# A decoder trunk on one core: projection pieces gathered behind Y, selection rounds shifted into the recurrence

## The reference

```
x = x + 0.5 * swiglu(rms_norm(x))
h = rms_norm(x); P = h @ W_in          # split by columns into the groups' q, k, v, ...
A: sparse attention, 6 heads x 64: index scores, top-128 keys per query, softmax with bias
B: gated delta rule, 6 heads x 64, chunks of 64 tokens, convolution, decay, output norm
C: attention into 256 memory tokens, 4 heads x 64
x = x + concat(A, B, C) @ W_out
x = x + 0.5 * swiglu(rms_norm(x))
```

```
v_new = u - w @ S;  o = q @ S + attn @ v_new;  S = decay * S + k^T @ v_new
```

## Time and profile before

| what | us |
|---|---|
| median of 3 runs (lowest to highest) | 2200.27 (2198.32 to 2202.68) |
| the profiled execution: its time | 2206.89 |
| its span, first to last instruction | 2205.1 |
| TensorE busy | 2179.1 (99%) |
| VectorE busy | 1079.1 (49%) |
| ScalarE busy | 772.6 (35%) |
| GpSimd busy | 380.1 (17%) |

### The profile page before, as it was taken

The page is one execution under the profiler, slowest core; times in us unless marked ns, Lnnn a source line. Parts: engine busy times, 40 slices in busy tenths (PEclk is TensorE's granted clock), DMA queues, the critical chain, the costliest instruction groups (busy, mean ns, idle before and its releaser), DMA issues.

```text
span 2205.1 us, 33287 instructions
## 1 busy us (share of the span) xinstructions
PE 2179.1 (99%) x13849; PEld 1762.6 (80%) x13849; DVE 1079.1 (49%) x1481; ACT 772.6 (35%) x1046; POOL 380.1 (17%) x319
## 2 busy tenths in 40 slices
PE   9999999999999999999999999999999999999999
PEld 7888888777777888888888888887777778888887
DVE  5333333789747544343343333338796465333322
ACT  5222223474335332222232222234743353222211
POOL 0111012005223410101111110120141134111000
PEclk9999999999999999999999999999999999999999
DMA  5222233221011222223222222232211012322232
GB/s 189 95 95 95 88 105 112 97 96 32 31 67 39 77 96 95 95 90 105 93 96 97 99 103 89 93 128 80 93 41 60 29 39 77 114 95 95 91 101 76
DMA packets 30651, 192.43 MB, mean 87 GB/s; under 512 B 3216, under 2 KB 5392, under 8 KB 11984
## 3 DMA queue, kind: packets, MB, share of 16 engines
q1 hardware_dynamic: 30160, 189.80, 25.5%
q10 hardware_dynamic: 384, 1.07, 0.1%
HBM read 188.64 MB, written 2.10 MB: 86 GB/s over the span
## 4 chain that ended last, share of the span: by engine, by line
PE 90%; DVE 7%; ACT 2%; issue 1%; DMA 0%; SPq 0%; DVEq 0%; ACTq 0%
PE psum L872 26%; PE psum L874 26%; PE psum L873 26%; PE psum L1290 2%; PE psum L1152 1%; PE psum L1003 1%; PE psum L1274 1%; PE psum L1167 1%; DVE wl L1707 1%; PE psum L1263 1%; DVE acc L1790 1%; PE psum L1237 1%; PE psum L1205 1%; DVE XL L1722 1%; PE psum L1199 1%
## 5 line engine op out<-in xcount | busy, mean ns | idle before, releaser
L872 PE MATMUL psum<-XH,wh 128*128 128x512 f32 x1904 | 764.2, 401 | 4.9 <-DVE wl L1707 1.8
L874 PE MATMUL psum<-XH,wl 128*128 128x512 f32 x1904 | 744.5, 391 | 0.0
L873 PE MATMUL psum<-XL,wh 128*128 128x512 f32 x1904 | 744.0, 391 | 0.0
L872 PEld LDWEIGHTS psum<-XH,wh 128*128 128x128 f32 x1904 | 358.7, 188 | 94.2 <-issue 14.8
L874 PEld LDWEIGHTS psum<-XH,wl 128*128 128x128 f32 x1904 | 358.8, 188 | 75.9
L873 PEld LDWEIGHTS psum<-XL,wh 128*128 128x128 f32 x1904 | 359.1, 189 | 73.8 <-issue 4.3
L1715 DVE TENSOR_TENSOR wl<-raw,wh 128x2048 fp32r<-128x2048 f32 x88 | 201.8, 2293 | 159.4 <-ACT wh L1360 159.4
L872 PE MATMUL psum<-HH,wh 128*128 128x512 f32 x704 | 273.9, 389 | 0.0
L873 PE MATMUL psum<-HL,wh 128*128 128x512 f32 x704 | 273.9, 389 | 0.0
L874 PE MATMUL psum<-HH,wl 128*128 128x512 f32 x704 | 273.9, 389 | 0.0
L1355 ACT ACTIVATE wh<-raw 128x2048 fp32r<-128x2048 f32 (+1 forms) x84 | 157.3, 1872 | 307.5 <-PE psum L874 307.3
(11 more groups left out here) (256 smaller groups left out, 2143.4 us busy)
## 6 DMA issues: line engine op xcount, KB each, us to landing
raw<-weights SPq DMA_DIRECT2D x143, 1024.0 KB, 5.0
raw<-weights SPq DMA_DIRECT2D x32, 896.0 KB, 4.6
xT<-xt SPq DMA_DIRECT2D x4, 512.0 KB, 6.6
memT<-memt SPq DMA_DIRECT2D x2, 1024.0 KB, 4.9
out<-xT SPq DMA_DIRECT2D x8, 256.0 KB, 5.8
stripsA<-strip_table SPq DMA_DIRECT2D x2, 768.0 KB, 6.8
raw<-weights SPq DMA_DIRECT2D x2, 512.0 KB, 6.8
stripsB<-strip_table SPq DMA_DIRECT2D x2, 512.0 KB, 7.4
```

The source lines that it names most:

```text
L872: pe.matmul(out_ap, a_hi, b_hi, start=first, stop=False)
L873: pe.matmul(out_ap, a_hi, b_lo, start=False, stop=False)
L874: return pe.matmul(out_ap, a_lo, b_hi, start=False, stop=last)
```

## The change

Only `_order` changes. In the Y and X steps `pull` is now called with 2.04 behind Y and not at all behind X; it was called with 1.02 behind each (behind "w" it stays 1.02). A selection round stands behind X and W, where it stood behind each step of Y, X and W but the last four. Eight rounds are thus fewer in the inversion; they stand in the recurrence behind each r1, which is behind the scaled values U on VectorE. As `later` counts calls of `pull`, the steps of the head norms and splits move too: they stand behind Y steps and W only.

```diff
--- before.py
+++ after.py
@@ -311,16 +311,18 @@
 
     for i, step in enumerate(INVERSION):
         order.append(step)
-        if i < len(INVERSION) - 4 and step != ("kq", 2):
+        if i < 9 and step != ("kq", 2) or step[0] in ("x", "w"):
             sel(1)
         if i < 9:
             pull(0.7 if i < 6 else 1.3)
-        else:
-            pull(1.02)
+        elif step[0] != "x":
+            pull(2.04 if step[0] == "y" else 1.02)
         if i == 0:
             put(("vt", 2), ("vt", 3))
     for step in RECURRENCE:
         order.append(step)
+        if step[0] == "r1":
+            sel(1)
         if step in FILLED:
             pull(0.92)
     assert all(name == "v" and b == 3 for name, b, _, _ in fill) and not later
```

## The result

The changed kernel took 2207.51 us (median of 10 runs, 2203.14 to 2213.93), the kernel before beside it 2200.16 (10 runs, 2198.32 to 2203.24): a ratio of 1.0027, 95% interval 1.0017 to 1.0036. The time lies inside the range of 2196 to 2209, but not at 2201.8: the difference was +7.35 us where +1.5 was forecast, and by the bound of 0.2% the kernel is slower, a case that had a chance of 0.15. The forecast's own range ended at 2205.5; the part above it, in which the measured time lies, was there for rival B, which did not happen. Two later timings of the same code gave 1.0021 (1.0013 to 1.0030) and 1.0014 (1.0003 to 1.0025).

What follows compares the result with a forecast made beforehand. TensorE bounds it, 90% of the chain. 18.7 (Y) + 29.9 + 4.3 + 18.6 + 0.6 + 7.0 = 79.1 us against 78.73 and 78.32; +1.5 us with g): 2201.8. Own range 2198 to 2205.5, with rivals 2196 to 2209.

Steps and rivals of the forecast that it cites:

- rival B: Clock falls to half speed in the emptied Y, X and W stretches: 2208.6 us if behind each W; chance 0.13.
- a) Switches: TensorE in the inversion: 14 bursts where there were 26, 29.9 instead of 32.3 us, so -2.4 us a layer.
- b) The hole behind X: Y waits uncovered for ScalarE's copy XX, 1.86 us after X instead of 1.56, at 10 places: +3.0 us a layer.
- c) Last X to W: W waits for the copy XTF without a piece between; 3.51 us twice, 7.0 against 5.0: +2.0 us a layer.
- d) ScalarE late at Y(0,5): Split and square queued on ScalarE from Y(0,4) delay the copy, due at 5.69, to about 6.3: +0.6 us.
- e) VectorE's stalls: X's waits for Y's subtraction, held up by work queued ahead on VectorE, go: -2.8 and -2.4 us in the layers.
- check sum: Priced steps of the inversion before the change: together 75.9 us, leaving 2.8 us of stalls in layer 0, 2.4 in layer 1.
- f) The recurrence: Eight selection rounds of 1.50 us fit VectorE's 31 idle us in the recurrence; cost on TensorE: nothing.
- g) The cut burst: The head sum of dk1 moves from "u" to r1(0,0), cutting one burst in two: +0.16 us a layer.
- Rival A: The copy behind X and the last X is not waited for: -7.7 us, 2192.6 us; chance 0.09.
- no change: Whole kernel: +1.5 us, within the 0.2% (4.4 us) that a measurement can't tell from nothing; chance 0.75.

Runs made afterwards that it cites:

- VectorE's copy: The changed kernel with VectorE instead of ScalarE copying XX at levels 1 and 3 of each group: 2206.25 us (1 run), inversions 81.66 and 81.24 us.
- the later split: The changed kernel with the high split of unit 13 one step later on ScalarE, at Y(0,5): 2201.28 us (1 run), inversions 80.00 and 79.37 us.
- the second round: Against the kernel with only the rounds moved, two selection rounds behind each r1 instead of one: 2202.03 us (1 run), recurrence 49.31 us.
- three later sets of before: The unchanged kernel, timed in three sets of runs: medians 2202.37 (35 runs), 2203.26 (23) and 2203.41 us (15).

## Why the prediction was right, and where it was not

**a) Switches: right.** Each burst of three comes back to X 3.81 behind Y, forecast 3.83, and in the kernel that keeps a piece behind each X, X to Y is 2.45, by the prediction's prices 1.56 + 0.90 = 2.46.

**b) The hole behind X: the step was right, its size was not, and this is the miss.** "A release costs about 0.05" was read off Y's subtraction and carried to the copy, where it is 0.14. X to Y is 1.95 for 1.86; over the 20 places that is 1.8 us. With it the forecast of 79.1 becomes 80.0, and 80.00 and 80.04 were measured. The 0.09 between them is the separate wait instruction that the Y step has and the X step has not. The other half of the step, that the copy starts 1.00 behind X, held at 0.99 to 1.00. The Trainium skill ("TensorE: Matmul & The Clock Gate", Single matmul latency) would have it at 0.89 by a formula that it gives for one bf16 matmul of the full array; VectorE's copy, starting at 0.99 as well, speaks for a delay ahead of either engine that the formula leaves out.

**c) Last X to W: right.** 3.52 for 3.51, and the piece put back there gave 1.5 us a layer.

**d) ScalarE late at Y(0,5): right.** 0.58 for 0.6; the later split took it away.

**e) VectorE's stalls: right that they go, in part wrong in what they are.** The 2.8 and 2.4 us left over by the check sum were all given to work queued ahead of the subtraction. Moving the rounds alone brought 1.33 and 1.22. Of the rest, the 0.45 at the first X is of that kind too, a round and a split that stay ahead of it. The four times 0.14 in group 1 are not: there the subtraction itself is longer than the one piece. Most of the 0.4 by which layer 0 had more was a pause of TensorE. It did not matter to the sum, since the sum was built from steps without stalls and the long bursts cover these small ones.

**f) The recurrence: right.** 47.25 for 47.23 and 47.26, with the forecast 27 busy us. How near the edge it is, the second round shows; and it shows that the slack was reckoned for the state alone, with the path through gzT and ScalarE left out.

**g) The cut burst: wrong, and small.** Moving the head sum from "u" to r1(0,0) was to cost 0.16 a layer. The recurrence, which holds both places, is only 0.02 longer: r1(0,0) has no matmul of its own, so the two bursts are one for TensorE, before and after.

**Rival A** fell at once; TensorE waits for the copy at every one of its places.

**Rival B, the clock.** It was not what happened: the changed stretches have ten holes of about 0.4 us or more behind X in each layer, and those at W, and show 1.00. The Trainium skill (same page, A second HAM failure mode: psum-queue depth-cycling) tells of a kernel in which short idles between groups of matmuls came so often that the clock swung; no trace here bears that out for these. The clock did bear on the sign in another way. The difference in time at equal clock is 3.7 us, under the 4.4 that the text set as the bound, so "no change" was a fair case, but the first timing measured 7.35. Of the other 3.6 the mean clock of the changed kernel's ten runs, 0.9963, explains part: the three later sets of before had 0.9966 to 0.9972, worth 0.6 to 1.7 us. The clocks of the runs of before in that first timing were not listed, so the rest stays open. The medians say where it lies: the changed kernel's 2207.51 is 1.0 and 1.4 us above its two repeats, and the 2200.16 of before is 2.2 to 3.3 below its three later sets. The two repeats, at +4.2 and +2.7, make chance the likely reason and show nothing against the 3.7. So both that the first difference was 7.35 and that the time still lay in the range are luck; the mechanism answers for 3.7.

**Where the 3.7 us are**: 1.6 and 1.7 in the two inversions (80.00 and 80.04 less 78.42 and 78.30), 0.04 in the recurrences; the remaining 0.3 is within the error of the fit.

**The better versions.** Both kernels are beaten by moving the rounds alone (0.9984, 0.9975 to 0.9993) and by moving them with one piece left behind each X (0.9986, 0.9976 to 0.9997); the two can't be told apart.

## What to carry to other kernels

A piece of other work between a producer and its consumer is worth the bare part of the copy between them, here 0.39 to 0.97 us (X to Y less 1.56), against 0.20 for the switch it costs: gather pieces only where they cover nothing. A bare wait also hands lateness on: what delayed one X step came back whole in the next Y step. When a wait is to become bare, take its price from start to start, with the release delay of that very wait: a wait that had an instruction of its own took 0.14 to 0.15 here and not 0.05. Work of an idle engine can be moved behind the operation that frees the critical path as long as it fits the tightest step with everything else that stands there, on every path that runs through that engine; the second round didn't.

## What the runs showed of the hardware

- TensorE starts 0.05 to 0.06 us after the end of what it waited for (VectorE's subtraction or state update, ScalarE's XTF and osq), and 0.14 to 0.15 after it where the trace has a wait instruction of its own ahead of the matmul (the copy XX by ScalarE or by VectorE, VectorE's kdc and AT). It goes with that instruction and not with engine or size; it was not tested by an edit.
- The copy's start stands 0.99 to 1.00 behind the start of the first block of an X step (24 matmuls of 64 x 64, 48 rows in the trace; a block of a Y step is 12 matmuls and 24 rows, and not 24 matmuls), for either engine.
- TensorE sometimes pauses 0.3 to 0.6 us within X(0,1) of layer 0, always at the same matmul, in four of the twelve traces, without a wait that the profile names.
- VectorE copies 128 x 768 float32 from PSUM in 0.96 us, ScalarE in 0.81.
- The falls of the clock to 0.50 come at fixed places of the program, 3.4 or 6.8 us long, but not in each execution. With them one kernel's time spreads over some 10 us; the times follow the mean granted clock at 1.86 us for 0.001. A comparison at equal clock tells 1 us apart where medians of 10 runs tell 2 to 3.
